# Recurrence's third block ahead of the stick attention's first step, gating and norm moved up by a step, their reciprocal apart, a root table loaded ahead

## What is computed

```python
def rg_lru(x, w_rg, b_rg, w_ig, b_ig, lam):
    r = sigmoid(block_diag_linear(x, w_rg, b_rg))
    i = sigmoid(block_diag_linear(x, w_ig, b_ig))
    log_a = -LRU_C * r * softplus(-lam)
    a = exp(log_a)
    bterm = sqrt(-expm1(2.0 * log_a)) * (i * x)
    h[t] = a[t] * h[t - 1] + bterm[t]            # written as a scan over time

def stick_breaking_attention(q, k, v):           # for blocks of 128 queries
    z = (q . k) / sqrt(dh);  mask = key < query
    log_1mb = where(mask, log_sigmoid(-z), 0)
    suffix = reverse_cumsum(log_1mb) - log_1mb
    att = where(mask, exp(log_sigmoid(z) + suffix), 0)
    return att . v

def second_block(...):
    ...
    y_lru = gelu(lru_g) * rg_lru(conv(lru_x), ...)
    y_att = stick_breaking_attention(q, k, v)
    y = concatenate([rms_norm(y_lru, g_lru), rms_norm(y_att, g_att)])
    x = x + y @ w_out
```

## Time and profile before

| | before |
|---|---|
| median of 3 runs | 1372.78 us (1372.58 to 1373.69) |
| profiled execution, device time | 1372.61 us |
| its span | 1370.6 us |
| instructions in the span | 18053 |
| PE busy | 1331.1 us, 97% |
| DVE busy | 790.1 us, 58% |
| POOL busy | 612.0 us, 45% |
| ACT busy | 549.5 us, 40% |

### The profile page before, as it was taken

One profiled execution on the slowest core, in us unless ns is written; L12 is line 12 of the kernel. 1 busy time (PEld: TensorE's weight loads), 2 busy tenths in 40 slices (PEclk: granted clock), 3 DMA queues, 4 the chain that ended last, 5 costly groups with the idle time before them and its releaser, 6 DMA issues. The chain is left out here.

```text
span 1370.6 us, 18053 instructions
## 1 busy us (share of the span) xinstructions
PE 1331.1 (97%) x6189; PEld 1079.0 (79%) x6189; DVE 790.1 (58%) x1097; ACT 549.5 (40%) x860; POOL 612.0 (45%) x299
## 2 busy tenths in 40 slices
PE   8998889999999999999999999899999999999997
PEld 6787766887678888888888777688788888888886
DVE  7788896632456777777533588677543333332222
ACT  5444776542343222323323254455442233232322
POOL 4597873332234444444444534132344444444441
PEclk9999999999999999999999999999999999999999
DMA  6122321221122222323322222111122222233222
GB/s 227 62 93 93 108 75 34 92 78 62 46 92 88 98 92 96 103 92 109 106 87 97 92 77 77 46 47 62 62 93 92 97 102 92 92 109 105 95 87 80
DMA packets 31875, 121.19 MB, mean 88 GB/s; under 512 B 3536, under 2 KB 3664, under 8 KB 31568
## 3 DMA queue, kind: packets, MB, share of 16 engines
q1 hardware_dynamic: 31536, 119.81, 25.9%
q10 hardware_dynamic: 288, 0.69, 0.2%
HBM read 118.40 MB, written 2.10 MB: 88 GB/s over the span
## 5 line engine op out<-in xcount | busy, mean ns | idle before, releaser
L625 POOL TENSOR_TENSOR weights_low<-weights_raw,weights_high 128x1024 fp32r<-128x1024 f32 (+1 forms) x204 | 526.4, 2581 | 725.3 <-ACT weights_high L703 725.1
L703 ACT CAST weights_high<-weights_raw 128x1024 fp32r<-128x1024 f32 (+1 forms) x202 | 221.9, 1099 | 504.7 <-PE acc L1736 475.1
L1736 PE MATMUL acc<-a_high,weights_high 128*128 128x512 f32 x976 | 390.5, 400 | 1.8 <-DVE a_low L1398 1.1
L1736 PE MATMUL acc<-a_high,weights_low 128*128 128x512 f32 x976 | 380.6, 390 | 0.0
L1736 PE MATMUL acc<-a_low,weights_high 128*128 128x512 f32 x976 | 380.3, 390 | 0.0
L1736 PEld LDWEIGHTS acc<-a_high,weights_high 128*128 128x128 f32 x976 | 183.7, 188 | 44.1 <-issue 3.7
L1736 PEld LDWEIGHTS acc<-a_low,weights_high 128*128 128x128 f32 x976 | 183.7, 188 | 39.3 <-issue 2.6
L1736 PEld LDWEIGHTS acc<-a_high,weights_low 128*128 128x128 f32 x976 | 183.5, 188 | 38.7
L1208 DVE TENSOR_TENSOR residual<-acc,residual 128x512 f32<-128x512 f32 (+1 forms) x63 | 43.3, 687 | 168.4 <-PE acc L1736 129.8
L1736 PE MATMUL acc<-h_high,weights_high 128*128 128x512 f32 x330 | 128.9, 391 | 0.0
L1736 PE MATMUL acc<-h_high,weights_low 128*128 128x512 f32 x330 | 128.4, 389 | 0.0
(11 more groups left out here) (384 smaller groups left out, 1932.8 us busy)
## 6 DMA issues: line engine op xcount, KB each, us to landing
weights_raw<-w SPq DMA_DIRECT2D x172, 512.0 KB, 3.2
weights_raw<-w SPq DMA_DIRECT2D x32, 704.0 KB, 4.1
residual<-xT SPq DMA_DIRECT2D x8, 256.0 KB, 6.1
out<-y_tok SPq DMA_DIRECT2D x4, 512.0 KB, 3.1
mem_raw<-memT SPq DMA_DIRECT2D x1, 1024.0 KB, 5.3
mem_tok<-mem SPq DMA_DIRECT2D x1, 1024.0 KB, 7.5
lru_weights<-blockdiag ACTq DMA_DIRECT2D x1, 512.0 KB, 3.3
sine<-positions SPq DMA_DIRECT2D x1, 256.0 KB, 6.7
```

The source lines that it names most:

```text
L625: g.tensor_tensor(weights_low[:, s, 0:cols], weights_raw[:, s, 0:cols], weights_high[:, s, 0:cols].bitcast(F32), ALU.subtract).then_inc(we ...
L703: a.copy(weights_high[:, s, 0:cols], weights_raw[:, s, 0:cols]).then_inc(weight_high, 1)
L1736: last = t_.matmul(acc[:, bank, 0:cols], w[:, s, wide], x_[:, k0 + k, 0:cols], start=start and k == opens and n == 0, stop=stop and k == c ...
```

## The change

The plan's third recurrence block, `("late", 2)`, leaves step 0 for a place ahead of it, behind the third reciprocal of the plan's end and ahead of tile 10. The fourth moves from behind step 2 to behind step 0. Gating (`hidden`), squares and their sum move up by a step each, most of them. The reciprocal gets an item of its own, `lru_factor`, behind step 9, a step ahead of the transposes that spread it (`att_factor` stands directly ahead of `att_spread`). A new item `att_table` at step 33 takes a root of a constant on ACT.

```diff
-        REC_PLAN += pieces(8) + [("late", 1)] + pieces(9) + [("turn", 0), ("inverse", 3)] + pieces(10)
+        REC_PLAN += pieces(8) + [("late", 1)] + pieces(9) + [("turn", 0), ("inverse", 3), ("late", 2)] + pieces(10)
...
-        AFTER = {0: [("late", 2)], 1: [("hidden", 0)], 2: [("late", 3)], 3: [("hidden", 1), ("square", 0)],
-                 4: [("hidden", 2)], 5: [("hidden", 3), ("square", 1)], 6: [("square", 2)],
-                 7: [("att_clear",), ("square", 3)],
-                 9: [("lru_sum",)], 10: [("lru_spread",)], 11: [("lru_scale",)], 12: [("lru_low",)],
-                 13: [("att_square", 0)], 20: [("att_square", 1)], 28: [("att_square", 2)]}
+        AFTER = {0: [("late", 3)], 1: [("hidden", 0)], 2: [("hidden", 1)], 3: [("square", 0), ("hidden", 2)],
+                 4: [("hidden", 3), ("square", 1)], 5: [("square", 2)], 6: [("att_clear",), ("square", 3)],
+                 8: [("lru_sum",)], 9: [("lru_factor",)], 10: [("lru_spread",)], 11: [("lru_scale",)],
+                 12: [("lru_low",)], 13: [("att_square", 0)], 20: [("att_square", 1)], 28: [("att_square", 2)]}
...
+            if step == 33:
+                REC_PLAN.append(("att_table",))
...
-        REC_PLAN += [("att_spread",)] + halves[3:4] + [("att_scale", 0), ("att_scale", 1)] + halves[4:]
+        REC_PLAN += [("att_factor",), ("att_spread",)] + halves[3:4] + [("att_scale", 0), ("att_scale", 1)] + halves[4:]
...
+                elif what == "att_table":
+                    own.step(a.activation(tok_root[:, 5:6], eps, ACT.Sqrt))
...
-                elif what == "lru_spread":
+                elif what == "lru_factor":
                     token_factor(RT["ylru"])
-                elif what == "att_spread":
+                elif what == "att_factor":
                     token_factor(RT["yatt"])
```

## The result

| | before | after |
|---|---|---|
| median of the runs | 1372.78 us | 1365.68 us |
| ratio to before | | 0.9944 (0.9933 to 0.9954) |
| profiled execution, device time | 1372.61 us | 1365.74 us |
| its span | 1370.6 us | 1363.9 us |

The change makes the kernel 7.1 us faster by the medians, 0.56% by the ratio. The forecast was 1367.6 us with a range of 1366.0 to 1369.7: the direction was right, the gain was larger than the range allows. (One of the six runs of the changed kernel took 4094.77 us and is left out.)

The account below looks back on a forecast made before the run. PE, busy for 97% of the span, was taken to bound the kernel. The terms -4.10 - 1.34 + 0.84 - 0.26 - 0.34 = -5.2 us took 1372.78 to 1367.6 us, range 1366.0 to 1369.7.

Parts of the forecast that it names:

- What bounds: Whole kernel: PE, busy 97% of the span, bounds it; gains come only where PE waits or runs at a lower clock.
- the main term: Spread of the recurrence's norm: PE's whole wait for the reciprocal, held on DVE behind step 10's scan, goes, -4.10 us.
- The clock's part: Transposes and matmuls behind the reciprocal's wait: they no longer run at the lower clock, -1.34 us.
- The blocks: Steps 0 and 1: moved third and fourth blocks hold POOL, POOL holds the scans, PE's wait at step 1 grows, +0.84 us.
- What remains is copy and handover: about 0.85 of 1.19, -0.34: PE's wait for the copy of q before step 8: shrinks as ACT's fourth square comes earlier, -0.34 us, bounds 0 to -0.34.
- The lateness of DVE at units 3 to 5: Steps 2 to 8: DVE has 3.0 us less to do, so step 5's multiply is in time at 863.02, -0.26 us.
- step 8 to step 9 with the sums: PE's stretch at step 8, the sums and step 9: forecast change 0.
- The attention's end: Spread of the attention's norm: PE's wait of 1.07 us stays, and `att_table` gains and costs nothing.
- rivals 1 to 4: Low clock at step 1, 1368.9 us (0.15); reciprocal partly ready, 1369.6 (0.13); no gain, 1372-1373 (0.06); DVE-POOL collisions, 1375.9 (0.03).
- Rival 5: Step 1: its wait goes as well if the shift moves POOL clear of the scan, -7.8 us, 1365.0 us; chance 0.07.
- the likeliest case: Whole kernel: forecast as worked out, spanning 1366.7 (no cost of the blocks) to 1368.4 us (+1.24, nothing for q); chance 0.56.
- rival 4: Steps 0 to 7: slower, DVE's and POOL's turns keep colliding, about +0.8 us, or +3.1 (1375.9 us) with a third; chance 0.03.

Follow-up runs that it names:

- the pair of split blocks: Changed kernel, attention's reciprocal ahead of the half tile, three or two of the fourth block's four instructions between the scans of steps 0 and 1: 1362.81 and 1363.63 us.

## Why the prediction fell short

**What bounds, and the main term: right.** The reciprocal had only stood in the wrong place on DVE. -4.26 against -4.10, shown from both sides: alone, with the clock, it gains 5.5 us of the stretch, and without it the change gains nothing that a measurement tells. The clock's part, -1.40 against -1.34, was right too. ACT's two loads and root took 869.14 to 872.00, 2.86 us, against 2.82 forecast. The Trainium skill (ScalarE: Activation LUTs, "What ACT_TABLE_LOAD costs") would have 2.66 us for each of the switches; here the root begins 0.02 us behind its load and the next load 0.01 behind the root, so no drain shows, and the row was the better guide. The reciprocal came at 873.34, not at 875: step 9's first sigmoid slipped by 0.5 us (872.02 against 871.54), not by 1.5, since PE was ahead by then.

**The blocks: right in mechanism and nearly in size.** +0.67 against +0.84. POOL held by a scan, the scan held by POOL, the two subtractions at "about 3.2" (3.10 and 3.02). The rule of the Trainium skill (SBUF — State Buffer, "SBUF: two separate sides") that the pair of ports is an exclusive lock for a whole instruction is borne out by the pair of split blocks: 0.45 us of work less took 1.32 us of waiting away.

**The step that failed: "What remains is copy and handover: about 0.85 of 1.19, -0.34", and "Bounds 0 to -0.34".** It measured -1.40, four times its own bound, and no wait for q was left where "0.8 to 0.9" were forecast. I had taken the end of the matmuls just ahead of the wait, 867.02, for the end of the tile that the copy reads. But between that tile and step 8 lie the value products and the first piece of the next tile: in the kernel before, the tile's last matmul began at 864.57 and the bank was whole at about 865.0. The copy could have begun up to 2.4 us earlier. It didn't, since ACT still had sigmoids to make, and then waited for DVE's addition and made the fourth square. With the chain a step ahead the copy begins as the tile ends (its last matmul at 865.26, the copy at 865.69) and nothing remains of the wait. The experiments show both sides: the third block alone leaves the wait for q at 1.20, the gating alone removes it.

**Two smaller terms were mis-sized.** The lateness of DVE at units 3 to 5 was worth 0.72, not 0.26, and step 8 to step 9 with the sums 0.43, not 0. With q's term as measured the sum would have been 1366.5 us, inside the range; these two take it to 1365.6. For one part the reason is how I read the idle column. It counts from the modelled end of the matmul before. PE starts the next one before that end: in after, the transposes at 863.77 begin 0.06 us behind the start of the instruction ahead of them, which lasts 0.22. So a wait costs more than its row shows. At 863.02 the one ahead had begun at 862.54, so 0.48 - 0.06 = 0.42 us were lost, not 0.26. At 848.01 it is 1.98 - 0.05 = 1.93, not 1.76, and at the copy of q, where the matmul ahead began at 866.62 and matmuls follow at 0.23, 1.59 - 0.23 = 1.36, not 1.19: 0.16 or 0.17 for each wait, the reciprocal's with them. Three waits, at 854.48, at 859.46 and in front of the sums, were so small that I had not priced them at all.

**The attention's end: right.** 1.07 us stay, `att_table` gains and costs nothing (stretch 138.93 without it).

**The rivals.** The clock did not fall behind the wait of 2.43 us at step 1, and the reciprocal was ready wholly, so rivals 1 to 4 are out. Rival 5, that the wait at step 1 goes, is out too; its time, 1365.0, was near the measured one by luck. Two of the prediction's figures don't follow from its terms: with +1.24 and nothing for q the likeliest case reaches 1368.3, not 1368.4, and the 0.03 for slower is the whole of rival 4, of which half is also counted within 0.2%.

**Which kernel is best.** The change with the attention's reciprocal ahead of its half tile, and with the fourth block behind step 2 (1362.97 us, 0.9924) or split (1362.81 us, 0.9922), is 2.7 to 2.9 us faster than the change by the medians, and 1.8 to 2.0 by the stretch, which the falls of the clock elsewhere don't touch. The five kernels that place the fourth block otherwise than the change does, with that reciprocal ahead, lie within 1 us, 1362.8 to 1363.8, which I don't call a difference: wherever the block goes between steps 0 and 2, some multiply of a unit comes 1 to 1.5 us late. An order that avoids it, for instance with the first gate behind step 2 as well, wasn't tried.

## What to carry to other kernels

An instruction of 0.17 us cost 5.5 us because it stood behind a wait that had nothing to do with it. Where engines walk a common list, look at each item whose result another engine needs at once, and ask what its predecessors on the same engine wait for; the same look found 1.3 us more at the attention's norm. When a wait is sized, find the instruction whose result is waited for and where its input was ready, not the one that happened to run last, and measure from start to start. Moving work off one step pays only if the step that takes it has room; parts of such a change can't be judged alone, as the gating shows, which by itself took one wait away and brought three, and in the change brought none.

## What the runs showed of the hardware that was not expected

- An instruction of DVE with one input, the tensor-scalar on 512 columns of float32 in SBUF, waits for POOL like those with two: 2.62 us instead of 0.42. (SBUF — State Buffer, "SBUF: two separate sides", in the Trainium skill says so of DVE's two-port modes; I had counted inputs alone, and no run here shows in which mode this one ran.) The trace of before had it already: the tensor-scalar at 803.55 took 1.40 us, and ended 0.28 behind POOL's subtraction. The additions from PSUM with one input in SBUF did not wait: at 953.20 of before one began 0.26 us behind POOL's start and took 0.68 us.
- Whether a DVE instruction gets ahead of POOL is settled by about a tenth of a microsecond, and it is worth the whole subtraction. In after a gate product began 0.10 us ahead of POOL (856.29) and took 0.69 us; in before an addition of the same size began 0.08 behind it (854.95) and took 2.88. By the starts of the profile the border isn't sharp: at 794.93 of before an instruction that shows 0.04 us ahead of POOL took 2.99 us.
- The clock behind the same wait of 4.10 us was low for different times in different executions: 0.88 on average over 14 us in one (before), 0.76 in the three others that have the wait, which took back 1.4 of the 2.1 us that the third block ahead had gained. A wait of 2.43 us was followed by no fall.
